# The residual after each LayerNorm: from GpSimd to VectorE, in four pieces behind other work

## What is computed

```python
for l in range(DEPTH):                       # DEPTH = 2
    mod = (cs @ ada_w[l] + ada_b[l]).reshape(bn, N_SUB, 3, D_MODEL)
    shift, scale, gate = mod[:, :, 0, None], mod[:, :, 1, None], mod[:, :, 2, None]
    u = x * (1.0 + scale[:, 0]) + shift[:, 0]
    x = _layer_norm(ALPHA * x + 0.5 * gate[:, 0] * _swiglu(u, ...), ln_g[l, 0], ln_b[l, 0])
    u = x * (1.0 + scale[:, 1]) + shift[:, 1]
    x = _layer_norm(ALPHA * x + gate[:, 1] * _hybrid_mixer(u, ...), ln_g[l, 1], ln_b[l, 1])
    u = x * (1.0 + scale[:, 2]) + shift[:, 2]
    x = _layer_norm(ALPHA * x + 0.5 * gate[:, 2] * _swiglu(u, ...), ln_g[l, 2], ln_b[l, 2])
```

## Time and profile before

| | us |
|---|---|
| median of 3 executions | 1263.16 (1261.47 to 1264.38) |
| the profiled execution | 1264.34, its span 1262.6 |

### The profile page before, as it was taken

The page is one execution under the profiler, slowest core; times in us unless marked ns, Lnnn a source line. Parts: engine busy times, 40 slices in busy tenths (PEclk is TensorE's granted clock), DMA queues, the critical chain, the costliest instruction groups (busy, mean ns, idle before and its releaser), DMA issues.

```text
span 1262.6 us, 17253 instructions
## 1 busy us (share of the span) xinstructions
PE 1114.2 (88%) x7041; PEld 970.7 (77%) x7041; DVE 934.6 (74%) x1353; ACT 398.1 (32%) x500; POOL 228.6 (18%) x213
## 2 busy tenths in 40 slices
PE   0899997979969789999978999897997888999994
PEld 0799986967855479999968999796776537999993
DVE  5688898876992688888778887988389458755554
ACT  1344432312131143333333443232122314343430
POOL 1000491032321110000020008702223112000003
PEclk9999997979988889999988999998998897999997
DMA  9798866865321468898964884786143036645530
GB/s 366 227 313 290 287 214 233 267 177 171 67 96 35 144 222 287 285 318 281 318 198 159 307 283 163 265 298 146 67 100 100 5 142 234 218 171 199 200 133 34
DMA packets 197010, 253.19 MB, mean 201 GB/s; under 512 B 41984, under 2 KB 145732, under 8 KB 195908
## 3 DMA queue, kind: packets, MB, share of 16 engines
q1 hardware_dynamic: 196932, 252.09, 59.6%
HBM read 251.03 MB, written 1.05 MB: 200 GB/s over the span
## 4 chain that ended last, share of the span: by engine, by line
PE 72%; DVE 17%; issue 4%; POOL 3%; DMA 2%; ACT 1%; SPq 0%; DVEq 0%; POOLq 0%; ACTq 0%
PE PS L482 13%; PE PS L484 13%; PE PS L483 12%; PE PS L507 6%; PE PS L511 6%; PE PS L510 6%; PE PS L581 5%; PE PS L742 3%; PE PS L464 2%; DVE arena L1159 2%; DMA w_in_ring<-in_ffn_w_dram 2%; DVE acc L863 1%; DVE w_in_lo L943 1%; DVE xn L1001 1%; PE PS L588 1%
## 5 line engine op out<-in xcount | busy, mean ns | idle before, releaser
L482 PE MATMUL PS<-u_hi,w_in_hi 128*128 128x256 f32 x1408 | 410.9, 292 | 13.9 <-DVE u_lo L894 13.9
L484 PE MATMUL PS<-u_hi,w_in_lo 128*128 128x256 f32 x1408 | 401.5, 285 | 0.0
L483 PE MATMUL PS<-u_lo,w_in_hi 128*128 128x256 f32 x1408 | 397.6, 282 | 0.0
L482 PEld LDWEIGHTS PS<-u_hi,w_in_hi 128*128 128x128 f32 x1408 | 268.6, 191 | 19.8 <-issue 18.5
L483 PEld LDWEIGHTS PS<-u_lo,w_in_hi 128*128 128x128 f32 x1408 | 268.2, 190 | 3.2 <-issue 1.9
L484 PEld LDWEIGHTS PS<-u_hi,w_in_lo 128*128 128x128 f32 x1408 | 269.6, 191 | 0.0
L943 DVE TENSOR_TENSOR w_in_lo<-w_in_ring,w_in_hi 128x2048 fp32r<-128x2048 f32 x88 | 207.1, 2354 | 42.2 <-ACT w_in_hi L1436 42.2
L1436 ACT ACTIVATE w_in_hi<-w_in_ring 128x2048 fp32r<-128x2048 f32 x88 | 167.5, 1908 | 45.4 <-DMA w_in_ring<-in_ffn_w_dram 27.6
L863 DVE SCALAR_TENSOR_TENSOR acc<-arena,cs,acc 128x512 f32<-128x512 f32 x217 | 168.6, 777 | 7.7
L507 PE MATMUL PS<-w_out_hi,h_parts 128*128 128x512 f32 x352 | 142.8, 406 | 15.4 <-DVE h_parts L937 15.4
L1444 ACT ACTIVATE w_out_hi<-w_out_ring 128x1024 fp32r<-128x1024 f32 x88 | 88.4, 1052 | 181.7 <-PE PS L511 181.7
(11 more groups left out here) (275 smaller groups left out, 1203.2 us busy)
## 6 DMA issues: line engine op xcount, KB each, us to landing
w_in_ring<-in_ffn_w_dram SPq DMA_DIRECT2D x88, 1024.0 KB, 7.7
arena<-in_ada_w_dram SPq DMA_DIRECT2D x31, 2048.0 KB, 8.2
w_out_ring<-in_ffn_w_dram SPq DMA_DIRECT2D x44, 1024.0 KB, 6.6
w_in_ring<-in_w_in_dram SPq DMA_DIRECT2D x8, 1024.0 KB, 5.7
w_out_ring<-in_w_out_dram SPq DMA_DIRECT2D x4, 1024.0 KB, 6.6
w_in_ring<-in_w_in_dram SPq DMA_DIRECT2D x2, 2048.0 KB, 9.2
w_out_ring<-in_w_out_dram SPq DMA_DIRECT2D x8, 512.0 KB, 4.3
w_in_ring<-in_w_in_dram SPq DMA_DIRECT2D x14, 256.0 KB, 5.4
```

The source lines that it names most:

```text
L482: pe.matmul(y, hi, u_hi[:, kt, :], start=(i == 0), stop=False)
L483: pe.matmul(y, hi, u_lo[:, kt, :], start=False, stop=False)
L484: mm = pe.matmul(y, lo[:, kt, half, :], u_hi[:, kt, :], start=False, stop=(i == KT - 1))
```

## The change

The multiplications and additions of the residual leave POOL, whose function `powers` keeps the two powers. DVE gets a function `residual(l, s, k)` of one operation: `k` = 0 and 2 multiply the halves by the gain, 1 and 3 add the bias. They are placed in four places:

- norm 0 of each layer: all four behind `s5_scan(0)` of that layer's mixer
- norm 1: one behind each of the chunks 0 to 3 of FFN 2, after the modulation block of that chunk
- norm 2 of layer 0: likewise behind chunks 0 to 3 of FFN 1 of layer 1
- norm 2 of layer 1: all four at the end

`ln_bc_used` is gone; ACT (`rows`) and SP (`load_ln`) wait for the matching count of `x_ready` instead.

```diff
--- before.py
+++ after.py
@@ -355,7 +355,7 @@
 
                 for ch in range(CHUNKS):
                     load_beside(0, ch)
-                sp.wait_ge(sem("ln_bc_used"), l * 3 + 1)
+                sp.wait_ge(sem("x_ready"), l * 6 + 2)
                 waited(sp)
                 load_ln(l, 0)
 
@@ -407,7 +407,7 @@
 
                 for ch in range(CHUNKS):
                     load_beside(1, ch)
-                sp.wait_ge(sem("ln_bc_used"), l * 3 + 3)
+                sp.wait_ge(sem("x_ready"), l * 6 + 6)
                 waited(sp)
                 load_ln(l, 2)
             for tt in range(2):
@@ -1002,6 +1002,19 @@
                                 ).then_inc(sem("xn_dve"), 1)
 
 
+            def residual(l, s, k):
+
+                n, tt = l * 3 + s, k // 2
+                if k % 2 == 0:
+                    v.wait_ge(sem("ln_bc_loaded"), (n + 1) * 32)
+                    v.wait_ge(sem("xn_act"), n * 2 + (tt + 1))
+                    if tt == 1:
+                        v.wait_ge(sem("xn_dve"), n + 1)
+                    v.tensor_tensor(x_sb[:, tt, :], xn[:, tt, :], ln_bc[:, 0, :], ALU.mult).then_inc(sem("x_step"), 1)
+                else:
+                    v.wait_ge(sem("x_step"), n * 2 + (tt + 1))
+                    v.tensor_tensor(x_sb[:, tt, :], x_sb[:, tt, :], ln_bc[:, 1, :], ALU.add).then_inc(sem("x_ready"), 1)
+
             v.sem_inc(sem("y_read"), 4)
             v.wait_ge(sem("cs_ready"), 1)
             for t in range(4):
@@ -1075,6 +1088,8 @@
 
                 for c in range(CHUNKS - 1):
                     ffn_chunk(l, 0, c)
+                    if l and c < 4:
+                        residual(l - 1, 2, c)
                     if c == 0:
                         v.wait_ge(sem("prm_turned"), l + 1)
                         v.tensor_copy(prm[:, :], PS[:, 7, 0:ROWS]).then_inc(sem("prm_ready"), 1)
@@ -1176,6 +1191,8 @@
                 s5_rotate_in(0)
                 s5_rotate_in(1)
                 s5_scan(0)
+                for k in range(4):
+                    residual(l, 0, k)
                 if l == 0:
                     ada_block(11, ada_w_2, "ada_2_loaded", 1, acc_2)
                 s5_rotate_in(2)
@@ -1379,6 +1396,8 @@
 
                 for c in range(CHUNKS):
                     ffn_chunk(l, 1, c)
+                    if c < 4:
+                        residual(l, 1, c)
                     if c == 6:
                         mod_cols((12, 30)[l], 2, 6, 0)
                     if c in (6, 8):
@@ -1388,6 +1407,9 @@
                     mod_ab(0, 2, l * 3 + 3, 5)
                     w_in_low(0, 0, ff_tile(l + 1, 0, 0))
                 deepnorm(l, 2)
+                if l + 1 == DEPTH:
+                    for k in range(4):
+                        residual(l, 2, k)
                 if l + 1 < DEPTH:
                     evac_uT(0, l * 24 + 24, l * 3 + 4, l * 2 + 2)
                     w_in_low(0, 1, ff_tile(l + 1, 0, 0) + 1)
@@ -1502,7 +1524,7 @@
                 z_copy(4, tokv[:, 0, :], 196)
                 z_copy(5, tokv[:, 1, :], 196)
                 z_copy(6, kbT[:, :])
-                a.wait_ge(sem("ln_bc_used"), l * 3 + 2)
+                a.wait_ge(sem("x_ready"), l * 6 + 4)
                 for n in (7, 8):
                     a.activation(rows[:, n - 7, :], z_in(n)[0:H, :], ACT.Identity, bias=gate_bias[:, n - 7:n - 6]
                                  ).then_inc(sem("z_read"), 1)
@@ -1633,27 +1655,16 @@
                 g.memset(m[0:64, P + 192:P + 256], NEG).then_inc(sem("const_step"), 1)
             g.memset(mask_a[64:128, P:P + 64], NEG).then_inc(sem("const_step"), 1)
             g.wait_ge(sem("const_step"), 19)
-            g.sem_inc(sem("ln_bc_used"), 1)
             g.wait_ge(sem("x_loaded"), 32)
             g.sem_inc(sem("x_ready"), 2)
 
-            def residual(l, s):
+            def powers(l, s):
 
                 n = l * 3 + s
                 for tt in range(2):
                     g.wait_ge(sem("var_ready"), n * 2 + (tt + 1))
                     g.tensor_tensor(rstd[:, tt:tt + 1], var_eps[:, tt:tt + 1], neg_half[:, 0:1], ALU.pow
                                     ).then_inc(sem("rstd_ready"), 1)
-                g.wait_ge(sem("ln_bc_loaded"), (n + 1) * 32)
-                for tt in range(2):
-                    g.wait_ge(sem("xn_act"), n * 2 + (tt + 1))
-                    if tt == 1:
-                        g.wait_ge(sem("xn_dve"), n + 1)
-                    g.tensor_tensor(x_sb[:, tt, :], xn[:, tt, :], ln_bc[:, 0, :], ALU.mult).then_inc(sem("x_step"), 1)
-                    g.wait_ge(sem("x_step"), n * 2 + (tt + 1))
-                    g.tensor_tensor(x_sb[:, tt, :], x_sb[:, tt, :], ln_bc[:, 1, :], ALU.add).then_inc(sem("x_ready"), 1)
-                g.wait_ge(sem("x_ready"), n * 2 + 4)
-                g.sem_inc(sem("ln_bc_used"), 1)
 
             for l in range(DEPTH):
 
@@ -1674,7 +1685,7 @@
                     g.wait_ge(sem("rot_step"), l * ROT_STEPS + (6 * k + 4))
                     g.tensor_tensor(cos_t[:, :, hi], t4[0], t4[1], ALU.subtract).then_inc(sem("rot_step"), 1)
                     g.tensor_tensor(sin_t[:, :, hi], t4[2], t4[3], ALU.add).then_inc(sem("rot_step"), 1)
-                residual(l, 0)
+                powers(l, 0)
 
                 for b in range(4):
                     tl = slice(2 * b, 2 * b + 2)
@@ -1707,8 +1718,8 @@
                 g.wait_ge(sem("varc_ready"), l + 1)
                 g.tensor_tensor(rstd_c, var_c, neg_half[:, :], ALU.pow).then_inc(sem("rstdc_ready"), 1)
 
-                residual(l, 1)
-                residual(l, 2)
+                powers(l, 1)
+                powers(l, 2)
 
 
 # ---- launch: one core; inputs and outputs as the reference has them ----
```

## The result

The changed kernel took 1241.83 us, median of 4 runs (1240.4 to 1245.06), beside 1262.82 for the kernel before in the same comparison (4 runs, 1261.47 to 1264.38): ratio 0.9837, 95% interval 0.9815 to 0.9859. The profiled execution took 1241.87 (span 1240.1), so 22.5 less than that of before with 1264.34 (span 1262.6). By the medians 21.0 us are saved. The traces show 1.5 more, because the profiled execution of before lay 1.5 over its median and that of after on its own. The forecast was 1239.4 with 23.8 saved, the range 1234 to 1249.

A forecast was written before the change was run, and what follows sets the result against it. The prediction took POOL's residual, holding up DVE before PE's FFN products, as the bound. Passages 15.9, mixer entries 2.4, tail 4.0 and clock 1.5 sum to 23.8: 1263.16 − 23.8 = 1239.4 us, range 1234 to 1249.

The forecast's parts named there:

- The lock: LayerNorm to FFN: POOL's residual, through shared ports, stretches DVE's xn (2.31 us), cast (2.42) and first `u_lo` pair (3.43).
- The FFN passages: Three passages into an FFN: products start 5.3 us earlier each, 15.9 together, with PE's seed as the next bound.
- The clock in the FFN stages: Behind the three FFN entries: less slow-clock time after the first product, 1.5 us saved in all.
- two rules: FFN entries: clock returns equally long after gapless work begins (3.3 us saved for three) or after the first product (0).
- The mixer entries: Two passages into the mixer: earlier xn saves 1.5 us in layer 1, at most 0.9 in layer 0, together 2.4.
- The rival of an early clock: Clock returns early everywhere, mixer passages included, some 1.8 us more than the 3.3: 1235.8 us, chance 11%.
- The tail: End of the kernel: DVE's four operations end at 1255.5 instead of POOL's 1259.50, 4.0 us saved (3.6 to 4.3).
- What DVE gets instead: Mixer and FFN chunks 0 to 3: the added 1.2 us DVE operations fit into DVE's idle time, cost 0.
- The rival of a slower kernel: FFN chunks: DVE's 1.2 us reaches PE and drops the clock, 42.6 us in all: 1282 us, chance 4%.
- The one of another wait in the place of `u_lo`: FFN passages: a weight part or transfer becomes the wait, only xn's 1.5 us stays each: 1252.3 us, chance 8%.

The follow-up runs named there:

- the useless work on GpSimd: Changed kernel plus four multiplications on GpSimd, on a tile nobody reads, in each of three FFN passages: 1256.02 us, ratio 0.9943.
- The late residual: Changed kernel with all residual but the last norm's back on GpSimd, started after u's split or batch 1's rotation: 1253.53 us, ratio 0.9937.
- tail only: Kernel before with only the last norm's residual moved to DVE, all others on GpSimd: 1259.41 us, ratio 0.9969.
- FFN passages on GpSimd: Changed kernel with the residual of the three norms leading into an FFN back on GpSimd: 1261.68 us, ratio 0.9989.
- the seed edit: Changed kernel with PE seeding accumulators ahead of the turn and xn's last half split 640 columns DVE, 384 ACT: 1241.48 us, ratio 0.9831.
- doubling the work: Changed kernel with each DVE residual operation behind chunks 0 to 3 of three FFNs preceded by another of the same size: 1242.48 us, ratio 0.9844.

## Why the prediction was right, and where not

**The lock: right.** POOL's 3% of the chain and DVE's long operations were read as one thing, and the useless work on GpSimd shows it with no data in common. By the rule of the Trainium skill (SBUF — State Buffer, Who interferes with whom) the two engines share a pair of ports that is held for a whole instruction; these traces agree, 2.31 against 0.55 us for the same scaling and 2.42 against 0.43 for the same cast. The rule also says that the one which issues first blocks the other. The late residual agrees: 4.37 us on GpSimd in place of 2.34, and 6.76 on DVE in place of 2.35. What the runs show by themselves is that these operations do not run side by side; that ports are the reason is the page's statement.

**The FFN passages: right in kind and size.** Forecast 5.3 each, measured 5.43, 5.42 and 5.43 from xn to the first product. After the change all three show 4.58. The steps hold one by one. The turn comes 441.24 − 438.78 = 2.46 behind xn before and 0.87 after: 1.6 where 1.50 was forecast. The cast gave 1.99 and the pair 2.15. The bound afterwards is the seed, as said. xn itself takes 0.55 and not 0.4 to 0.5, hidden behind ACT's 0.81.

**The clock in the FFN stages: right in sign, in part by another place.** Forecast 1.5. From the first product on, the clock stayed low for 4.7, 5.7 and 2.9 us before, and stays for about 3.2, 3.5 and 4.1 after. Half the difference is 1.25 us, with 0.75, 1.1 and −0.6 in the three. The forecast had one size for all, between two rules of which neither holds in all three, so that the sum is near is luck. In the first passage of the changed kernel a stretch that begins 1.4 us after its first product reads

```profile
444.00:446.00 2.00, 2.00 (x12) 2.00 (x11) 2.00 (x4) 1.98 (x2) 0.00 (x0) 0.55 1.02 401
```

where the earlier trace rows has 0.50 and 0.63, ending 4.7 behind the product. What had no step in the forecast is a stretch that the kernel before has in FFN 1 of layer 1, behind the waits of chunks 6 and 7:

```profile
812.00:814.00 2.00, 2.00 (x6) 1.62 (x5) 2.00 (x1) 0.00 (x0) 0.60 (x1) 0.50 1.10 348
814.00:816.00 2.00, 2.00 (x7) 1.55 (x7) 1.93 (x4) 0.00 (x0) 0.00 (x0) 0.67 0.03 8
```

(2.00 × 0.50 + 2.00 × 0.33 = 1.66 us lost), and the changed kernel in the same work

```profile
799.00:801.00 2.00, 2.00 (x10) 1.65 (x9) 2.00 (x1) 0.00 (x0) 0.41 (x1) 1.00 1.03 329
```

not. The ledger closes: 3 × 5.43 + 1.25 + 1.66 = 19.2 against 18.9 for the three stages. The last term had no step in the forecast. It goes with the change, and is not settled by it: the stretch stands in all five traces in which GpSimd works in or behind the FFN entries (before, tail only, FFN passages on GpSimd, useless work, late residual) and is missing in seven of the eight others, but the seed edit, which is as early, has it again. What decides it is open.

**The mixer entries: mis-sized, the term that failed.** Forecast 2.4, "1.5 us in layer 1" and "at most 0.9" in layer 0. The rows gave 1.55 at the first products in both, so the mechanism was there. In the stages it came to 0.1 and −1.1. In layer 0 the forecast reckoned with a transfer that stands still and a norm that stands still too; the norm came 0.7 earlier and the transfer did not come with it (19.09 us behind the norm before, 20.01 after), which left nothing of the 0.9. In layer 1 I ended the account at the entry and carried 1.5 to the end of the stage, although in its rivals the clock had been allowed to take back what an entry gains in the FFN passages. The rival of an early clock "in the mixer's passages too" had the sign wrong: there the clock came back relatively later, at a cost of 0.9, 0.45 and 2.9 − 1.7.

**The tail: right.** Forecast 4.0, measured 3.9. Timeline of DVE and of SP's queue at the end, which answers to the earlier trace rows:

```profile
1231.69 0.55 DVE L1001 TENSOR_SCALAR xn<-xn,rstd,nmr 128x512 f32<-128x512 f32 x1
1232.15 1.22 DVE L1013 TENSOR_TENSOR x_sb<-xn,ln_bc 128x1024 f32<-128x1024 f32 x1
...
1235.80 1.23 DVE L1016 TENSOR_TENSOR x_sb<-x_sb,ln_bc 128x1024 f32<-128x1024 f32 x1
...
1234.65 2.74 SPq L415 DMA_DIRECT2D out_dram<-x_sb  x2
```

**What DVE gets instead: right, with cover to spare.** The operations take 1.22 us each. Those in the mixer of layer 0 end at 299.67, and ACT's `rows`, written at 306.36, are released by PE and not by DVE:

```profile
306.36 0.46 ACT L1529 ACTIVATE ln_bc<-PS,gate_bias 4x256 f32<-4x256 f32 x1 [3.22 <-PE PS L581]
```

PE's waits for `h_parts` are 15.4 us in 5 times, as before, and doubling the work cost nothing. The rival of a slower kernel (1282) needed this cover to fail. The one of another wait in the place of `u_lo` (1252.3) needed a releaser other than PE, and there is none. One reading was not exact: in 664 to 830 us PE has, besides the two waits of the earlier trace rows, that for `u_lo` at the FFN entry, 3.8 us, which the sum counts elsewhere.

**The sum.** Forecast 15.9 + 2.4 + 4.0 + 1.5 = 23.8. In the trace: 18.9 in the FFN stages (17.4 forecast with the clock), −1.0 in the mixers (2.4), 3.9 in the tail (4.0), 0.7 in the start (0): 22.5. The miss of 3.4 in the mixers was made up to two thirds by a clock stretch (1.5 in the FFN stages) and by the start (0.7), so the total was nearer than its parts, and that was luck. By the medians the saving is 21.0, 2.8 under the forecast, because the trace of before lay 1.5 over its median.

## What to carry to other kernels

When an operation of DVE takes several times what the same line takes elsewhere in the trace, lay GpSimd's timeline beside it: the share of GpSimd in the chain, 3% here, says little, for its cost is booked under DVE's busy time. Where DVE is busy throughout, moving the GpSimd operation later mostly moves the collision: here it kept a quarter of the gain. On DVE it took half the duration and, behind waits of DVE, cost nothing. And a microsecond gained at the entry of a stage is to be followed to the end of that stage, past transfers and past where the TensorE clock comes back, before it is put into the sum.

## What the runs showed of the hardware that I had not expected

- Two engines that hold each other up both pay: GpSimd operations of 2.34 to 2.41 us took 4.37, 3.27 and 3.37 beside a busy DVE, and a DVE pair of 2.35 took 6.76.
- GpSimd's useless multiplication, which reads one tile as both inputs, takes 1.96 us and holds DVE as well.
- Without a DVE neighbour the residual on DVE costs 1.22 us an operation, half of GpSimd's 2.34 to 2.41, so where the stores wait for it, at the end, the move would save time even if nothing were locked; elsewhere `x_sb` is read only at the next norm.
- The granted TensorE clock can change a mixer stage of the same kernel by 2.7 us between executions (169.97 and 172.65), and an earlier start of a stage can end later (164.78 against 163.77 us with the entry 1.55 earlier). Differences under some 3 us between kernels of this kind are to be looked up in the granted clock first.
